# Two-layer attention and expert step: the last three projection blocks beside the first units, late conditioning products in stage 0

## The reference

```python
def run(x, c, pos, past_ckv, past_kr, past_bk, past_bv):
    for layer in range(2):
        mod = silu(c) @ ada_w[layer] + ada_b[layer]            # ada_w: (2, 1024, 6144)
        sh_m, sc_m, g_m, sh_f, sc_f, g_f = split(mod, 6)
        h = rmsnorm(x, norm_mix_w) * (1 + sc_m) + sh_m
        if layer == 0: out, ckv, kr = mla_mixer(h, ...)
        else:          out = band_mixer(h, k_all, v_all, ...)
        x = x + g_m * out
        h = rmsnorm(x, norm_ffn_w) * (1 + sc_f) + sh_f
        x = x + g_f * peer_ffn(h, p_w_q, p_subkeys, p_u, p_v)
        if layer == 0: k_all, v_all = shared_kv(x, c, ...)     # one more product for shift and scale
    return x, ckv, kr, k_all, v_all

def mla_mixer(h, ...):
    proj = h @ w_in                                            # 1024 x (384 + 256 + 32)
    c_q, c_kv, k_r = rmsnorm(proj[:384]), rmsnorm(proj[384:640]), proj[640:]
    q = rope(rmsnorm(c_q @ w_uq))                              # 384 x 16*96
    k_nope, v = (concat(past_ckv, c_kv) @ w_ukv)               # 256 x 16*(64+64)
    k = rope(rmsnorm(concat(k_nope, k_r)))
    return softmax(q k^T, chunk-causal) v @ w_o, c_kv, k_r

def peer_ffn(h, w_q, subkeys, u, v):
    q = (h @ w_q).reshape(n, 8, 2, 64)                         # w_q: 1024 x 1024, 4 MB
    top_s, top_i = top_k(q . subkeys, 16)                      # for each half
    best_s, idx = top_k(all 256 sums of the two halves, 16)
    a = gelu(h . u[idx])
    return sum(softmax(best_s) * a * v[idx])
```

## Time and profile before

| | us |
|---|---|
| median of 3 runs (4301.57 to 4315.13) | 4311.06 |
| the profiled execution | 4325.95 |
| its span | 4324.1 |
| first dot of stage 0 | 501.1 |
| first dot of stage 1 | 691.2 |
| granted TensorE clock, mean over the span | 0.795 |
| moved by DMA over the span | 1473.97 MB, 341 GB/s |

### The profile page before, as it was taken

The page is one execution under the profiler, slowest core; times in us unless marked ns, Lnnn a source line. Parts: engine busy times, 40 slices in busy tenths (PEclk is TensorE's granted clock), DMA queues, the critical chain, the costliest instruction groups (busy, mean ns, idle before and its releaser), DMA issues.

```text
span 4324.1 us, 31445 instructions
## 1 busy us (share of the span) xinstructions
PE 2654.6 (61%) x9649; PEld 968.8 (22%) x9649; DVE 2466.7 (57%) x5988; ACT 414.4 (10%) x1032; POOL 2458.8 (57%) x2322
## 2 busy tenths in 40 slices
PE   6977535555464464546456674665547666667689
PEld 2434322221121111212122231222213211111122
DVE  2442896785575456645764555775566556644410
ACT  1322111100010000110010010011001100000000
POOL 0000235667776756665775565566666666666665
PEclk8987757777686676777667777877768889999999
DMA  8763467999998999989998997999999999999999
GB/s 338 253 223 117 156 219 263 337 352 337 349 396 331 360 416 383 381 339 359 398 391 335 404 395 280 386 364 357 349 408 403 360 344 355 369 373 379 372 366 339
DMA packets 481567, 1473.97 MB, mean 341 GB/s; under 512 B 61193, under 2 KB 134873, under 8 KB 480729
## 3 DMA queue, kind: packets, MB, share of 16 engines
q0 software_dynamic: 332160, 1208.77, 73.6%
q1 hardware_dynamic: 123848, 251.13, 15.9%
q10 hardware_dynamic: 25392, 12.06, 1.0%
HBM read 1444.78 MB, written 28.57 MB: 341 GB/s over the span
## 4 chain that ended last, share of the span: by engine, by line
DMA 26%; POOL 25%; PE 18%; DVE 14%; issue 12%; another core or an unknown queue 4%; ACT 1%; SPq 0%; DVEq 0%; ACTq 0%; POOLq 0%
DMA A<-in_uv,A 24%; POOL A L1683 13%; POOL A L1703 12%; PE P L813 8%; DVE A L1518 6%; PE P L734 1%; PE P L704 1%; PE P L588 1%; PE P L610 1%; PE P L691 1%; DVE A L1405 1%; PE P L535 1%; DVE A L1402 1%; DVE A L1404 1%
## 5 line engine op out<-in xcount | busy, mean ns | idle before, releaser
L813 PE MATMUL P<-A 128*32 128x512 f32 x4608 | 1327.2, 814 | 1249.3 <-DMA A<-in_uv,A 1116.6
L1683 POOL DMA_INDIRECT A<-in_uv,A x1152 | 1224.5, 1063 | 1022.1 <-DVE A L1518 551.9
L1518 DVE CUSTOM_DVE_ANT_0 A<-A 128x1024 f32<-128x1024 f32 x900 | 1094.0, 1224 | 790.8 <-DMA A<-in_uv,A 733.6
L1703 POOL DMA_INDIRECT A<-in_uv,A x1152 | 1222.1, 1061 | 553.7 <-issue 306.1
L813 PEld LDWEIGHTS P<-A 128*32 128x32 f32 x4608 | 267.7, 133 | 2125.0 <-issue 1667.2
L1518 DVE CUSTOM_DVE_ANT_0 A<-P,A 128x1024 f32<-128x1024 f32 x252 | 306.8, 1224 | 294.4 <-DMA A<-in_uv,A 243.5
L830 PE MATMUL P<-A 128*128 128x512 f32 (+1 forms) x480 | 233.0, 629 | 22.5 <-DMA A<-in_w_kv 13.5
L704 PE MATMUL P<-A 128*128 128x128 f32 (+2 forms) x832 | 157.2, 325 | 130.0 <-DVE A L1368 76.4
L734 PE MATMUL P<-A 128*128 128x512 f32 (+1 forms) x320 | 198.4, 752 | 3.1 <-DMA A<-in_w_oA 2.5
L691 PE MATMUL P<-A 96*64 96x320 f32 (+9 forms) x320 | 155.8, 590 | 35.5 <-DMA A<-qA_scratch 16.3
L718 PE MATMUL P<-A 128*64 128x128 f32 (+2 forms) x832 | 137.0, 299 | 58.4 <-ACT A L1055 57.6
(11 more groups left out here) (171 smaller groups left out, 2060.2 us busy)
## 6 DMA issues: line engine op xcount, KB each, us to landing
A<-in_ada_w SPq DMA_DIRECT2D x28, 2048.0 KB, 9.6
A<-in_w_kv SPq DMA_DIRECT2D x80, 512.0 KB
A<-in_uv,A POOLq DMA_INDIRECT x2304
A<-in_w_oA SPq DMA_DIRECT2D x40, 512.0 KB
A<-in_w_q SPq DMA_DIRECT2D x40, 512.0 KB
A<-in_w_oB SPq DMA_DIRECT2D x40, 512.0 KB
A<-in_p_w_q SPq DMA_DIRECT2D x2, 4096.0 KB, 13.5
G<-mod_scratch SPq DMA_DIRECT2D x8, 512.0 KB, 8.2
```

Of the source, the lines that this page charges most:

```text
L813: ins = pe.matmul(Y[32 * j:32 * j + 32, b, :], spread[:, w:w + STRIDE], row[:, 512 * b:512 * b + 512], start=(m == 0), stop=(m == STRIDE - ...
L1518: dve.tensor_tensor_reduce(u_slot[b], row, u_slot[b], 1.0, 0.0, ALU.mult, ALU.add, dots[u % 2][:, j:j + 1]).then_inc(sem("dots_done"), 1)
L1683: pool.indirect_dma_start(u_slot[at % U_SLOTS], None, table, bass.IndirectOffsetOnAxis(ap=expert[u % 2][:, j:j + 1], axis=0)).then_inc(sem ...
L1703: pool.indirect_dma_start(row, None, table, bass.IndirectOffsetOnAxis(ap=expertT[u % 3][:, n:n + 1], axis=0)).then_inc(sem(name), 16)
```

## The change

1. *Conditioning.* Three groups (12 pieces, `EARLY = 3`) stay ahead, in blocks 0 to 2 (`PIECES = [2, 2, 4]` and four before block 0). The other 16 pieces go through two slots `late_w` that lie where V gathers land later, in stage 0: on PE two pieces each after the 2nd, 4th and 6th step of selection (0,1), then two after heads 3, 6, 9, 12 and 15 of attention (0,2). DVE adds their biases after dots 28 and 46 and at the end of the stage. Their result `late_mods` lies in the area of `spread`; so POOL clears `spread` ahead of the first V gather of stage 1, once `mods2` is stored. Gains of layer 1 are made in stage 2, before in stage 1.
2. *Projections.* Blocks 0 to 3 stay ahead; blocks 4 to 6 (`project_rest`) run between attention (0,0), selection (0,0), picks (0,0) and attention (0,1), on PE, ACT and DVE by one table, `RAMP` (a attention (0,0), s selection, c picks, b attention (0,1), p a step of a block, e exponentials). For that a block lives in fewer banks: `banks` gives each use one in turn of 4, 5, 6, 7, from block 4 on of 6 and 7, and each use waits until the one before on its bank is emptied. ACT copies raw keys and raw latents to SBUF first, the norms read them there. Keys and queries are stored in two halves through one pair of buffers (`staged`).
3. *Weights.* `w_pq` shares its memory with the projections' buffers. Selection (0,0) takes it in eight chunks of 512 KB through `mid_ring` (`rows_of_selection`); it is loaded whole once more after the last projections are stored, for selection (0,1).
4. Loads of constants stand in another order, the new rows and piece 3 earlier; the gathers of the last unit count on the semaphores of the slots.

The diff, cut to its core:

```diff
 ADA_GROUPS = ADA_BLOCKS // 4
-PIECES = [2, 2, 4, 4, 4, 4, 4]
+PIECES = [2, 2, 4]
+EARLY = 3
+RAMP = ["aaapaaaapaaaaapaaaapaaaaa", "spspspspss", "ccpccpccpccpccpccpccpccpeccc",
+        "bcbcpbcbcpbcbcpbcbcpbcbcpbcbcpbcbcpbcbcpebcbcbcpbb"]
...
+        late_w = [A[:, at:at + 4096].rearrange("p (q n) -> p q n", q=4) for at in (4096, 8192)]
...
+        banks, before = {}, {}
+        for i, x in enumerate(uses):
+            cycle = (4, 5, 6, 7) if i <= uses.index(("keysT", 3, 3)) else (6, 7)
+            banks[x] = cycle[i % len(cycle)]
+            before[x] = [y for y in uses[:i] if banks[y] == banks[x]][-1:]
...
             def pieces(lo, hi):
 
                 for p in range(lo, hi):
-                    if p >= 3:
+                    if 3 <= p < 4 * EARLY:
                         sp.wait_ge(sem("ada_used"), p - 2)
+                    elif p >= 4 * EARLY + 2:
+                        sp.wait_ge(sem("ada_used"), p - 1)
...
-            pieces(6, 14)
-            pass_mods(1, 3, "mods1")
-            pieces(14, 4 * ADA_GROUPS)
-            pass_mods(3, ADA_GROUPS, "mods2")
+            pieces(6, 4 * EARLY)
+            pass_mods(1, EARLY, "mods1")
...
-                if u == 0:
-
-                    sp.wait_ge(sem("lat_stored"), 32 * TILES)
-                    load(w_pq, a["p_w_q"][0].rearrange("(p c) n -> p c n", c=C), "w_pq_loaded")
-                    load(skT, a["skT"][0], "skT_loaded")
+                if u == 2:
+                    pieces(4 * EARLY, 4 * EARLY + 8)
                 for g in range(C):
...
                     out_rows(g)
+                    if u == 2 and g in (0, 1, 2, 4):
+
+                        n = 4 * EARLY + 8 + 2 * (0, 1, 2, 4).index(g)
+                        pieces(n, n + 2)
+
+            def rows_of_selection():
+
+                sp.wait_ge(sem("values_summed"), HEADS)
+                for c in range(C):
+                    if c == 3:
+                        sp.wait_ge(sem("out_chunks"), C)
+                    elif c >= 4:
+                        sp.wait_ge(sem("pq_chunks"), c - 3)
+                    load(mid_ring[c % 4], a["p_w_q"][0].rearrange("(p c) n -> p c n", c=C)[:, c, :], f"mid{c % 4}_loaded")
+                sp.wait_ge(sem("pq_multiplied"), 2)
...
-            sp.wait_ge(sem("vA_stored"), 16 * len(KEYS_A))
-            sp.wait_ge(sem("kA_stored"), 16 * len(KEYS_A))
-            sp.wait_ge(sem("qA_stored"), 16 * TILES)
+            projections_stored(3)
             attention(0, 0)
...
+                if u == 1:
+                    projections_stored(4)
+                elif u == 2:
+
+                    projections_stored(len(KEYS_A))
+                    sp.wait_ge(sem("lat_stored"), 32 * TILES)
+                    sp.wait_ge(sem("q_turned"), 4 * TILES)
+                    sp.wait_ge(sem("keys_turned"), 4 * len(KEYS_A))
+                    load(w_pq, a["p_w_q"][0].rearrange("(p c) n -> p c n", c=C), "w_pq_loaded")
...
+                    biases_of_mods(EARLY, ADA_GROUPS, "biases_loaded")
                 attention(layer, k)
+                if u == 2:
+                    pass_mods(EARLY, ADA_GROUPS, "mods2")
...
-            for _ in attention(0, 0):
-                pass
-            for _ in select(0, 0):
-                pass
-            for _ in attention(0, 1):
-                pass
+            def project_rest():
+
+                for n in range(4, len(KEYS_A)):
+                    yield from project(n, iter(()), 0)
+
+            steps = {"a": attention(0, 0), "s": select(0, 0), "b": attention(0, 1), "p": project_rest(), "c": iter(()), "e": iter(())}
+            for part in RAMP:
+                for x in part:
+                    pull(steps[x])
             turn_experts(0, 0)
...
-                if stage:
+                if stage == 0:
+                    pieces = mod_pieces(4 * EARLY, 4 * ADA_GROUPS)
+                    for n in range(6):
+                        pull(ready)
+                        if n % 2 == 1:
+                            pull(pieces, 2)
+                    for n in range(HEADS):
+                        pull(heads)
+                        if n >= 3 and n % 3 == 0:
+                            pull(pieces, 2)
+                else:
...
-                if stage == 1:
+                if stage == 2:
                     gains(("mix1", "ffn1", "kv"), "mods2_loaded")
...
                     if stage == 0:
+                        if j in (28, 46):
+                            sum_mods(EARLY if j == 28 else EARLY + 1)
...
-            pool.memset(spread, 0.0).then_inc(sem("spread_zeroed"), 1)
+            pool.memset(late_mods, 0.0).then_inc(sem("cleared"), 1)
...
+                        if i == 0 and stage == 1:
+
+                            pool.wait_ge(sem("mods2_stored"), 16 * 4)
+                            pool.memset(spread, 0.0).then_inc(sem("spread_zeroed"), 1)
                         gather_v(*place(stage - 1), i)
```

More of the change, by code:

```diff
@@ L580, in multiply_latents, with multiply_values @@
-            def multiply_latents(i):
+                    pe.wait_ge(sem("latents_copied"), 2 * (n - 1))
+                b = bank("keys", n, half)
+                for c in range(2):
+                    ins = pe.matmul(P[0:r, b, :], latents_of(n, c), w_ukv[:, c, 512 * half:512 * half + 512], start=(c == 0), stop=(c == 1))
+                ins.then_inc(sem("keys_multiplied"), 1)
+            def multiply_values(n, half):
+                r, b = block_rows(n), bank("values", n, half)
+                for c in range(2):
+                    ins = pe.matmul(P[0:r, b, :], latents_of(n, c), w_ukv[:, c, D + 512 * half:D + 512 * half + 512], start=(c == 0), stop=(c == 1))
+                ins.then_inc(sem("v_multiplied"), 1)
@@ L658, in _ @@
-            turn_queries(TILES - 1, 0)
-            turn_queries(TILES - 1, 1)
-            pe.wait_ge(sem("qT_copied"), 2 * TILES)
-            pe.wait_ge(sem("keysT_copied"), 2 * len(KEYS_A))
-            pe.wait_ge(sem("mods_summed"), ADA_GROUPS)
+            for n in range(4):
+                for _ in project(n, pieces, PIECES[n] // 2 if n < EARLY else 0):
+                    pass
             def attention(layer, k):
@@ new lines, in square_keys, with copy_values @@
+                act.activation(T1[0:r, 0:D].rearrange("p (h e) -> p h e", h=HEADS), kn_r.rearrange("p (h e) -> p h e", h=HEADS)[0:r, :, 0:NOPE],
+                               ACT.Square).then_inc(sem("keys_squared"), 1)
+            def copy_values(n):
+                r, (s, b) = block_rows(n), block(n)
+                if n:
+                    act.wait_ge(sem("vA_stored"), 16 * n)
+                for half in range(2):
+                    act.wait_ge(sem("v_multiplied"), 2 * n + half + 1)
+                    act.copy(Vst[0:r, 512 * half:512 * half + 512], P[0:r, bank_of("values", n, half), :]).then_inc(sem("v_copied"), 1)
+                act.wait_ge(sem("v_copied"), 2 * n + 2)
+                store(vA_dram[s][:, 0:r, b, :].rearrange("g p n -> p g n"), Vst[0:r, :].rearrange("p (g n) -> p g n", g=C), "vA_stored")
@@ L1028, in _ @@
-                if 0 <= ahead < TILES:
-                    copy_latents(ahead)
+                yield
+                for x in range(4):
+                    if now >= 0:
+                        copy_raw_queries(now, x)
+                    if x == 1:
+                        yield
                 if now >= 0:
                     square_queries(now)
-                copy_keys(n, 0)
-                copy_keys(n, 1)
+                yield
+                if new:
+                    copy_latents(ahead)
@@ L1665, in _ @@
                         pass
+                if stage == 0:
+                    sum_mods(EARLY + 2)
+                    sum_mods(EARLY + 3)
             weigh(*place(UNITS - 1))
```

594 lines of the change are left out of this document (352 added, 242 removed).

## The result

| | before | changed |
|---|---|---|
| median, us (16 runs each) | 4307.67 | 4328.59 |
| ratio, 95% interval | 1 | 1.0047 [1.0031, 1.0063] |
| the profiled execution's span | 4324.1 | 4315.8 |
| first dot of stage 0 | 501.1 | 446.9 |
| stage 0 | 190.1 | 264.2 |

A forecast was written before the change was run, and what follows sets the result against it. Gathers were taken to hold the kernel from the first expert dots on, something else the ramp; ramp -61, stage 0 +35 +4 +3 +4 and stage 1 +11 gave -4 on 4311, so 4307 us (own range 4292 to 4322, overall 4260 to 4346).

The follow-up runs named there:

- no late pieces: Changed kernel without loads, products and sums of the 16 late pieces, second load of selection weights kept; ratio 0.9888 to the kernel before, stage 0 197.0 us.
- single pieces: Changed kernel with one pair of late pieces ahead of head 0, then one piece after each of heads 0 to 13; ratio 0.9957, again 0.9959, to the kernel before.
- own queue: Changed kernel, but ScalarE issues the last eight late pieces on its own queue instead of SyncE; ratio 0.9996 to the kernel before, stage 0 239.8 us.
- longer clearing: Changed kernel with GpSimd clearing `spread` twelve more times ahead of stage 1's first V gather; ratio 1.0109 to the kernel before, stage 1 343.7 us.

## What to carry to other kernels

When work is moved under another stage, the bytes that it adds are the smaller question: ask for each transfer that waits for a slot what is queued behind it on its queue and when that is needed. Price the moved work at both places, and at the place where its result is awaited: here the 16 products cost some 33.5 us in front and 68 late, or 25 to 43 late once they were issued in the order of need. And read an account of a change at the point where its last effect ends, not at the end of two profiles that differ by more than the change.

## What the runs showed of the hardware

- A bulk load slows the first gather beside it. SyncE issued 4 MB 3.5 us ahead of the first dot (no late pieces); dot 4, whose gather GpSimd issued 1.5 us after the first dot, started 11.5 us after it. Before, when SyncE issued nothing there, it started after 5.8 us, and with 512 KB after 9.3 (rows, biases, keys and queries are still loaded beside it).
- The ramp is not the same from one execution to the next. The stretch 164 to 264 us of the same program (single pieces, and again on another chip) had a mean granted clock of 0.73 in one and 0.82 in the other, and the first dot came at 455.8 and 446.2. The chip alone does not make it: own queue, with the same ramp, ran on the chip of the first with 0.81 and 444.4. The first and the second:

```profile
164.00:264.00 100.00, 90.39 (x327) 47.12 (x325) 32.43 (x87) 34.56 (x103) 1.07 (x2) 0.73 0.34 100
```

```profile
164.00:264.00 100.00, 85.69 (x344) 45.07 (x344) 36.61 (x91) 36.94 (x109) 1.07 (x2) 0.82 0.39 121
```

- Of the four chips of the experiments, one ran the kernel before at 4181 us and the others at 4302 to 4316. The trace on the fast one (longer clearing) is level with that of the changed kernel up to 3390 us; behind that it takes 831.2 us for 925.6, with 402 GB/s for 361.
